# Building gate one-hots token by token with per-partition scalars, multiplying 256 columns at once, and adding the halves on VectorE

## The reference, cut to what matters

```python
def block(hb):                       # per token: 8 heads, 16 experts each = 128 picks
    ...
    sc, ci = lax.top_k(cand, PEER_TOPK)
    e = i1[ci // 16] * PEER_NKEYS + i2[ci % 16]      # expert = (first key, second key)
    g = jax.nn.softmax(sc, axis=-1)
    a = jax.nn.gelu(einsum('td,ted->te', hb, u[e]))
    return einsum('te,ted->td', g * a, v[e])
```

## Time and profile before

| | us |
|---|---|
| median of three runs | 2211.7 |
| the profiled execution, its own time | 2211.71 |
| its span, first to last instruction | 2209.8 |
| TensorE busy | 2155.0 |
| VectorE busy | 1125.3 |
| ScalarE busy | 608.4 |
| the 1024 gate products of 128 columns with the high part or the rest, first and last start | 882.4 to 1341.2 |

### The profile page before, as it was taken

One profiled execution on the slowest core, in us unless ns is written; L12 is line 12 of the kernel. 1 busy time (PEld: TensorE's weight loads), 2 busy tenths in 40 slices (PEclk: granted clock), 3 DMA queues, 4 the chain that ended last, 5 costly groups with the idle time before them and its releaser, 6 DMA issues.

```text
span 2209.8 us, 30856 instructions
## 1 busy us (share of the span) xinstructions
PE 2155.0 (98%) x12924; PEld 1464.6 (66%) x12924; DVE 1125.3 (51%) x2470; ACT 608.4 (28%) x1026; POOL 180.9 (8%) x272
## 2 busy tenths in 40 slices
PE   6999999989899999999999999999999999999999
PEld 4733435668688888898898988888444444444444
DVE  4197636452687993555554442230554554554452
ACT  0102122210123233333333333232233233233231
POOL 0001000000054650000000000000400000000000
PEclk9999969559999999999999999999999999999999
DMA  3232512001121343444444444542967667556551
GB/s 139 79 84 95 185 43 91 1 3 58 39 77 44 130 173 116 173 173 192 191 192 192 191 173 188 187 162 108 323 192 241 207 199 236 200 183 227 199 182 39
DMA packets 131690, 326.21 MB, mean 148 GB/s; under 512 B 22888, under 2 KB 88664, under 8 KB 115168
## 3 DMA queue, kind: packets, MB, share of 16 engines
q1 hardware_dynamic: 128080, 316.34, 40.1%
q0 software_dynamic: 3472, 7.91, 1.5%
HBM read 250.95 MB, written 73.27 MB: 147 GB/s over the span
## 4 chain that ended last, share of the span: by engine, by line
PE 96%; DVE 3%; DMA 1%; ACT 0%; issue 0%; SPq 0%; DVEq 0%; ACTq 0%
PE psum L1696 31%; PE psum L1741 29%; PE psum L1465 27%; PE psum L1717 5%; PE psum L1534 1%; PE psum L1471 1%; DMA g_in<-d_gate 0%; DVE sdm L1089 0%; DMA xT<-in_xT 0%; DVE v_lo L1388 0%; DVE rstd L846 0%; DVE mtmp L845 0%; DVE mtmp L844 0%; DVE hraw L1118 0%; DVE w_f L1397 0%
## 5 line engine op out<-in xcount | busy, mean ns | idle before, releaser
L1696 PE MATMUL psum<-h_hi,u_hi 128*128 128x260 bf16 x2048 | 395.1, 274 | 0.7 <-ACT Ssb L752 0.7
L1696 PE MATMUL psum<-h_lo,u_hi 128*128 128x260 bf16 x2048 | 393.7, 273 | 0.0
L1696 PE MATMUL psum<-h_hi,u_lo 128*128 128x260 bf16 x2048 | 393.5, 273 | 0.0
L1741 PE MATMUL psum<-w_hi,v_hi 128*128 128x512 bf16 x1024 | 388.1, 379 | 1.2 <-DVE w_lo L1404 1.2
L1741 PE MATMUL psum<-w_hi,v_lo 128*128 128x512 bf16 x1024 | 388.1, 379 | 0.0
L1741 PE MATMUL psum<-w_lo,v_hi 128*128 128x512 bf16 x1024 | 388.1, 379 | 0.0
L1255 DVE TENSOR_TENSOR u_lo<-u_raw,u_hi 128x1024 bf16<-128x1024 f32 x128 | 152.5, 1218 | 367.0 <-ACT u_hi L760 367.0
L1397 DVE TENSOR_TENSOR w_f<-a_in,g_in 128x512 f32<-128x512 f32 x128 | 87.9, 686 | 297.6 <-PE psum L1741 245.9
L1696 PEld LDWEIGHTS psum<-h_hi,u_hi 128*128 128x128 bf16 x2048 | 200.4, 98 | 29.7 <-issue 0.8
L1696 PEld LDWEIGHTS psum<-h_lo,u_hi 128*128 128x128 bf16 x2048 | 198.1, 97 | 31.0
L1696 PEld LDWEIGHTS psum<-h_hi,u_lo 128*128 128x128 bf16 x2048 | 198.2, 97 | 30.8
(11 more groups left out here) (311 smaller groups left out, 2175.8 us busy)
## 6 DMA issues: line engine op xcount, KB each, us to landing
u_raw<-in_uT SPq DMA_DIRECT2D x32, 2048.0 KB, 10.3
v_raw<-in_v SPq DMA_DIRECT2D x32, 2048.0 KB
d_act<-act_f SPq DMA_DIRECT2D x32, 1024.0 KB, 4.8
d_gate<-stage SPq DMA_DIRECT2D x16, 2048.0 KB, 6.3
a_in<-d_act SPq DMA_DIRECT2D x32, 1024.0 KB
g_in<-d_gate SPq DMA_DIRECT2D x32, 1024.0 KB
wr<-in_w SPq DMA_DIRECT2D x13, 2048.0 KB, 7.7
kv<-in_ck SPq DMA_DIRECT2D x24, 256.0 KB, 4.3
```

The lines of the kernel that those rows point to most:

```text
L1696: mm = pe.matmul(upair[n % 2][:, f, 0:HALF], w[g % 2][:, k, c * P:(c + 1) * P], hs[:, k, halves[f]], start=(k == 0 and x == 0), stop=(k == ...
L1741: mm = pe.matmul(ybank[m], w[g % 2][:, c, m * P:(m + 1) * P], z[g % 2][:, c, :], start=(g == 0 and c == 0 and x == 0), stop=(g == NG - 1 a ...
```

## The change

Three things are rewritten. VectorE builds each one-hot for one token with TENSOR_SCALAR: the 128 keys along the row (`keyrow`, bf16), compared with a column of `tables` (now f32) as a per-partition scalar, and for `gateL` multiplied by a second per-partition scalar. That is three instructions of 128 columns a token, 24 a pair, instead of four of 1024. The outputs are packed, so that TensorE reads its operands without a stride, and high part and rest lie side by side: one product of 256 columns a token, 8 a pair instead of 16 of 128. The two halves are no longer added by accumulation in PSUM. A quad now takes two banks, `gate_parts` gives its halves, ScalarE copies the high half into `stage`, and VectorE adds the other half in place (`add_gate_parts`), GATE_LAG = 2 loop indices behind. There are now two bank pairs, and quad q waits for the add of quad q - 2. `gl_ev` is signalled by VectorE. AT_V moves from 96 to 98.

```diff
-AT_V = 96
+AT_V = 98
+GATE_LAG = 2
...
-    gateL = [put(f"gateL{b}", [P, 2, 2, P, 4], BF16, ...
-    oneL = [put(f"oneL{b}", [P, 2, P, 4], BF16, ...
+    tables = put("tables", [P, 4, SEQ], F32, D0)
+    keyrow = put("keyrow", [P, P], BF16, c0 + 1024)
+    gateL = [put(f"gateL{b}", [P, 8, 2, P], BF16, ...
+    def gate_parts(q):
+        pair = pa[:, 4 + 2 * (q % 2):6 + 2 * (q % 2), :]
+        return pair.rearrange("p j (t x e) -> p x e (j t)", t=2, x=2)
...
-                A(stage[n % 2][:, :, at:at + 4], gbank[q % 4].rearrange("p (t e) -> p e t", t=4), ACT.Copy
-                  ).then_inc(gl_ev, 1)
+                A(stage[n % 2][:, :, at:at + 4], gate_parts(q)[:, 0, :, :], ACT.Copy).then_inc(gl_high, 1)
...
             def gate_rows(u):
-                each = lambda row: tables[:, row, 8 * u:8 * u + 8].rearrange(...)
-                tt(oneL[u % 2][:, :, :, :], keys, each(0), ALU.is_equal).then_inc(gl_one, 1)
+                row = lambda x, t: tables[:, x, 8 * u + t:8 * u + t + 1]
                 if u >= PRING:
                     v.wait_ge(gl_mm, 2 * (u - PRING + 1))
-                tt(oneR[u % PRING][:, :, :, :], keys, each(1), ALU.is_equal).then_inc(gl_R, 1)
-                v.wait_ge(gl_one, u + 1)
-                for part in range(2):
-                    tt(gateL[u % PRING][:, part, :, :, :], oneL[u % 2][:, :, :, :], each(2 + part), ALU.mult
-                       ).then_inc(gl_L, 1)
+                for t in range(8):
+                    ts(oneR[u % PRING][:, t, :], keyrow[:, :], row(1, t), None, ALU.is_equal)
+                    ts(gateL[u % PRING][:, t, 0, :], keyrow[:, :], row(0, t), row(2, t), ALU.is_equal, ALU.mult)
+                    ins = ts(gateL[u % PRING][:, t, 1, :], keyrow[:, :], row(0, t), row(3, t), ALU.is_equal, ALU.mult)
+                ins.then_inc(gl_L, 1)
+
+            def add_gate_parts(q):
+                n = q // QUADS
+                v.wait_ge(gl_high, q + 1)
+                at = 4 * (q % QUADS)
+                part = stage[n % 2][:, :, at:at + 4]
+                tt(part, part, gate_parts(q)[:, 1, :, :], ALU.add).then_inc(gl_ev, 1)
...
                 if 0 <= n - AT_GATES < NPAIRS:
                     gate_rows(n - AT_GATES)
+                if 0 <= n - AT_GATES - GATE_LAG < NPAIRS:
+                    add_gate_parts(2 * (n - AT_GATES - GATE_LAG))
+                    add_gate_parts(2 * (n - AT_GATES - GATE_LAG) + 1)
...
             def gates(q):
-                if q >= 4:
-                    pe.wait_ge(gl_ev, q - 3)
+                if q >= 2:
+                    pe.wait_ge(gl_ev, q - 1)
                 for t in range(4):
-                    for part in range(2):
-                        mm = pe.matmul(gbank[q % 4][:, t * P:(t + 1) * P], oneR[u % PRING][:, q % 2, :, t],
-                                       gateL[u % PRING][:, part, q % 2, :, t], start=(part == 0), stop=(part == 1))
+                    at = (t % 2) * 2 * P
+                    mm = pe.matmul(gbank[2 * (q % 2) + t // 2][:, at:at + 2 * P], oneR[u % PRING][:, 4 * (q % 2) + t, :],
+                                   gateL[u % PRING][:, 4 * (q % 2) + t, :, :], start=True, stop=True)
```

More of the change, by code:

```diff
@@ L158, in trunk_and_peer @@
     c0 = hs0 + HT
-    tables = put("tables", [P, 4, SEQ], BF16, c0)
     s_int = put("s_int", [DB * H, 3, TOPK], U32, c0 + 4160)
@@ L285, in trunk_and_peer @@
     act_f = [put(f"act_f{b}", [P, GC, NT], F32, C0 + 8320 * b) for b in range(2)]
-    keys4 = put("keys4", [P, P, 4], BF16, D0)
-    gateL = [put(f"gateL{b}", [P, 2, 2, P, 4], BF16, E0 + 4096 * b) for b in range(PRING)]
-    oneL = [put(f"oneL{b}", [P, 2, P, 4], BF16, E0 + 16384 + 2048 * b) for b in range(2)]
+    tables = put("tables", [P, 4, SEQ], F32, D0)
+    g_high = put("g_high", [P, SEQ], BF16, c0)
+    keyrow = put("keyrow", [P, P], BF16, c0 + 1024)
+    gateL = [put(f"gateL{b}", [P, 8, 2, P], BF16, E0 + 4096 * b) for b in range(PRING)]
     T0 = F0 + 8192
     stage = [put(f"stage{b}", [P, NKEYS, TB], F32, T0 + 16384 * b) for b in range(2)]
-    oneR = [put(f"oneR{b}", [P, 2, P, 4], BF16, T0 + 32768 + 2048 * b) for b in range(PRING)]
+    oneR = [put(f"oneR{b}", [P, 8, P], BF16, T0 + 32768 + 2048 * b) for b in range(PRING)]
     assert T0 + 32768 + 2048 * PRING <= W0
@@ L344, in trunk_and_peer @@
     qz_zero, s_used, rank_steps, one_hot, looked = sems("qz_zero scores_used rank_steps one_hot_ranks looked_up")
-    keys_set, tb_made, tb_read, gl_one, gl_L, gl_R, gl_mm, gl_ev = sems(
-        "keys_set tb_made tb_read gl_one gl_L gl_R gl_mm gl_ev")
+    keys_set, tb_made, tb_read, gl_L, gl_mm, gl_high, gl_ev = sems(
+        "keys_set tb_made tb_read gl_L gl_mm gl_high gl_ev")
     g_stored, a_stored, as_stored = ([sem(f"{n}{b}") for b in range(2)] for n in ("g_stored", "a_stored", "as_stored"))
@@ L1342, in _ @@
                 v.wait_ge(tb_made, i + 1)
-                v.tensor_copy(tables[:, 2, t], bk[:, 2 * P:3 * P]).then_inc(tb_high, 1)
-                v.tensor_copy(tables[:, 0, t], bk[:, 0:P])
-                v.tensor_copy(tables[:, 1, t], bk[:, P:2 * P])
+                v.tensor_copy(g_high[:, t], bk[:, 2 * P:3 * P]).then_inc(tb_high, 1)
+                v.tensor_copy(tables[:, 0:3, t], bk[:, 0:3 * P].rearrange("p (x t) -> p x t", x=3))
                 v.wait_ge(tb_high, i + 1)
-                tt(tables[:, 3, t], bk[:, 2 * P:3 * P], tables[:, 2, t], ALU.subtract).then_inc(tb_read, 1)
+                tt(tables[:, 3, t], bk[:, 2 * P:3 * P], g_high[:, t], ALU.subtract).then_inc(tb_read, 1)
             n64 = DB * H
@@ L1368, in _ @@
             v.wait_ge(hs_done, KT)
-            do(v.tensor_copy(keys4[:, :, :], iota.unsqueeze(2).to_broadcast([P, P, 4])), keys_set)
-            keys = keys4[:, :, :].unsqueeze(1).to_broadcast([P, 2, P, 4])
+            do(v.tensor_copy(keyrow[:, :], iota), keys_set)
             def gate_rows(u):
-                each = lambda row: tables[:, row, 8 * u:8 * u + 8].rearrange(
-                    "p (q t) -> p q t", q=2).unsqueeze(2).to_broadcast([P, 2, P, 4])
-                tt(oneL[u % 2][:, :, :, :], keys, each(0), ALU.is_equal).then_inc(gl_one, 1)
+                row = lambda x, t: tables[:, x, 8 * u + t:8 * u + t + 1]
                 if u >= PRING:
                     v.wait_ge(gl_mm, 2 * (u - PRING + 1))
-                tt(oneR[u % PRING][:, :, :, :], keys, each(1), ALU.is_equal).then_inc(gl_R, 1)
-                v.wait_ge(gl_one, u + 1)
-                for part in range(2):
-                    tt(gateL[u % PRING][:, part, :, :, :], oneL[u % 2][:, :, :, :], each(2 + part), ALU.mult
-                       ).then_inc(gl_L, 1)
+                for t in range(8):
[9 more added lines that the diff above has]
+                tt(part, part, gate_parts(q)[:, 1, :, :], ALU.add).then_inc(gl_ev, 1)
             def v_low(g, s):
@@ L1710, in gates @@
                 if q % 2 == 0:
-                    pe.wait_ge(gl_R, u + 1)
-                    pe.wait_ge(gl_L, 2 * (u + 1))
-                if q >= 4:
-                    pe.wait_ge(gl_ev, q - 3)
+                    pe.wait_ge(gl_L, u + 1)
+                if q >= 2:
+                    pe.wait_ge(gl_ev, q - 1)
                 for t in range(4):
-                    for part in range(2):
-                        mm = pe.matmul(gbank[q % 4][:, t * P:(t + 1) * P], oneR[u % PRING][:, q % 2, :, t],
-                                       gateL[u % PRING][:, part, q % 2, :, t], start=(part == 0), stop=(part == 1))
+                    at = (t % 2) * 2 * P
+                    mm = pe.matmul(gbank[2 * (q % 2) + t // 2][:, at:at + 2 * P], oneR[u % PRING][:, 4 * (q % 2) + t, :],
+                                   gateL[u % PRING][:, 4 * (q % 2) + t, :, :], start=True, stop=True)
                 mm.then_inc(gl_mm, 1)
```

## The result

| | before | after |
|---|---|---|
| median, us | 2211.7 | 2315.8 (2312.7 to 2327.3) |
| the profiled execution, its own time | 2211.71 | 2315.89 |
| its span | 2209.8 | 2314.0 |
| TensorE busy | 2155.0 | 2114.8 |
| VectorE busy | 1125.3 | 1359.1 |

The changed kernel takes 1.050 times as long, with a 95% interval of 1.044 to 1.056. By the last row the stage grew by 118.6 us, and the whole by only 104.2. Executions of the kernel before take either 2191 to 2198 us or 2205 to 2212, those of the changed kernel 2313 to 2316 or, once, 2327, and the profiled ones are a long one before and a short one after.

What follows compares the result with a forecast made beforehand. TensorE, busy 98%, was taken to set the pace. Rounds 114.4, start 15.6 and end -0.5 summed to 129.5 us, on 2211.7 giving 2341; range 2280 to 2430, chance 0.81.

Steps and rivals of the forecast that it cites:

- S: VectorE's one-hots for a pair: 8 instructions with one scalar and 16 with two, 5.04 us, against 2.40 before.
- D: One VectorE index: subtraction 1.15, one-hots 5.04 and two adds of 0.60, 7.39 us, slower than TensorE's step of 6.27.
- the standstill: TensorE idle before its gates once in four steps, until VectorE's add ends: 1.78 + 1.15 + 5.04 + 0.69 = 8.66 us.
- rounds' surplus: Between first and last pause, 14 rounds of four steps at 37.25 us against 29.08, 8.17 more each: 114.4 us.
- if both hold together: VectorE's one-hots: one source and bf16 each halve column time, giving spacings 0.170 and 0.230; 0.033 more if only one holds.
- The start and the end together: Stage edges: reaching the gates of step 31 costs 15.6 us more, the three steps after step 87 take 0.5 less.
- The wait that is added: TensorE's gates wait for VectorE's add two indices later, behind `u_low` and 24 `gate_rows` instructions: 8.66 us once in four steps.
- The clock: After each pause TensorE runs about 4.7 us at half clock, losing 2.35 us, hidden in the rounds by VectorE's slower pace.
- Dearer pieces: Rival: VectorE's new instructions or adds cost more; S of 5.84 gives 2390 us, 7.44 gives 2490; range 2375 to 2490, chance 0.22.
- cheap ones: Rival: VectorE's scalars are hidden, S = 2.64, TensorE sets the pace outside pauses; 2277 us, range 2250 to 2310, chance 0.13.
- faster: Rival: VectorE's add is done before TensorE asks, so TensorE keeps its 64 us saving: 2148 us, chance 0.03.
- the fixed 0.084 us: On VectorE, an instruction starts 0.084 us before the one ahead has ended; used to turn durations into spacings.

Runs made afterwards that it cites:

- the smaller S: Changed kernel, but from the fifth pair on the low half of `gateL` isn't built, 16 instructions a pair instead of 24: 2284.0 us, ratio 1.037.
- half-and-half kernel: Changed kernel with GATE_LAG = 1, `u_low` later at every fourth index, even quads 256 columns and an add, odd quads accumulated in PSUM: 2171.3 us, ratio 0.985.
- the four that only accumulate: Changed kernel with two 128-column products a token accumulated in PSUM, no adds: 2175.6 us; also with `u_low` later 2137.9, strided weights 2180.2, strided moving operand 2236.8.

## Why the prediction was right, point by point

The forecast was 2341 us, and 2315.8 was measured: the right sign, and 25 us too high. The named places and terms of the argument all appeared, nearly all a little smaller.

| term | forecast | measured | from |
|---|---|---|---|
| gates block | 0.90 | 0.87 | 890.19 above |
| one-scalar, two-scalar spacing | 0.170, 0.230 | 0.16, 0.225 | 1015.39, 1015.55, 1015.78, 1016.00 |
| S, 24 instructions | 5.04 | 4.87 | 1015.39 to 1020.26 |
| an add, apart | 0.60 | 0.595 | 1020.26 to 1021.45, two |
| D, a VectorE index | 7.39 | 7.20 | 1014.25 to 1021.45 |
| the standstill | 8.66 | 8.61 | 1012.47 to 1021.08 |
| its pieces | 1.78 + 1.15 + 5.04 + 0.69 | 1.78 + 1.14 + 4.87 + 0.82 | 1012.47, 1014.25, 1015.39, 1020.26, 1021.08 |
| gates and `up` after it | 8.6 | 8.39 | 1021.08 to 1029.47 |
| gates and `up` before it | 1.05 + 5.37 | 6.32 | 1006.15 to 1012.47 |
| a round | 37.25 | 36.53 | 984.55 to 1021.08 |
| `u_high` waited for, a round | about 8 | 7.65 | 1014.25 |
| rounds' surplus, 14 | 114.4 | 104.3 | 14 x (36.53 - 29.08) |
| stage in all | 129.5 | 118.6 | first gelu to last |

The prediction counts the standstill from when TensorE could have started its next product. The last two products of `up` ahead of it are this row of TensorE's timeline:

```profile
1012.25 0.38 PE L1707 MATMUL psum<-h_hi,u_lo 128*128 128x260 bf16 x2
```

They start 0.112 us apart, so the next could have started at 1012.47. The 8.45 us in the brackets count from 1012.63, where the trace has the last product's end.

**Where the 25 us are.** The first 10.9 are in the stage, and nearly all of them in the rounds. The 24 instructions were sized 0.17 us too long, and S stands four times in a round: 4 x 0.17 = 0.68 of the 0.72 by which a round is shorter. That was the step "if both hold together, 128 bf16 columns stream as long as 64 f32 ones": the case was right, and the duration taken from one row of 254 ns was too coarse. The rest of the 0.72 nearly cancels: gates and `up` before the standstill are 0.10 shorter, the subtractions and adds 0.07, and TensorE starts 0.82 us after the add's start and not 0.69, which is 0.13 longer. The start and the end together were forecast at 15.6 - 0.5 = 15.1 and took 118.6 - 104.3 = 14.3.

The other 14.4 us are not of the change. The first gelu of the changed kernel stands at 721.49 and that of the kernel before at 736.43. This early part ran at another clock; this is the stretch from 300 to 350 us, before and after (length; busy of the engines; granted clock; DMA). The kernel before:

```profile
300.00:350.00 50.00, 50.00 (x140) 20.25 (x139) 25.99 (x76) 9.36 (x31) 0.00 (x0) 0.66 0.20 64
```

The changed kernel:

```profile
300.00:350.00 50.00, 50.00 (x208) 22.61 (x207) 33.65 (x97) 12.64 (x41) 0.00 (x0) 1.00 0.20 64
```

It is not the code that sets it. With the smaller S, whose early part is that of the changed kernel, this stretch is at 0.72 and the first gelu at 733.49. The stretch is at 1.00 with GATE_LAG = 1, with the adds first and in the half-and-half kernel as well, and at 0.66 or 0.67 in the four that only accumulate. Against the shortest of the three times of the kernel before, 2194.89 us, the changed kernel's 2315.8 is 121 us more, about what the stage says. What decides the clock of the early part is open. The prediction took the profiled time as the base and named no such term; a range for it of 15 us downwards would have belonged there.

**The wait that is added** was the core, and it held. TensorE stood idle at 16 places, as forecast (the first at step 28, then 15). The four runs on it bracket the mechanism: with the add an index earlier the pause goes, without S ahead of the add it is shorter by S (3.59 us are left), with eight of its 24 instructions missing it is shorter by 8.45 - 6.67 = 1.78, those instructions' own 8 x 0.225, and being faster than TensorE on the average doesn't remove it.

**The clock** behaved much as the earlier trace rows had it. TensorE's granted clock in stretches of 2 us around the pause:

```profile
1012.00:1014.00 2.00, 0.63 (x6) 0.30 (x4) 0.00 (x0) 1.33 (x2) 0.00 (x0) 1.00 0.00 0
1014.00:1016.00 2.00, 0.00 (x0) 0.00 (x0) 1.75 (x5) 2.00 (x3) 0.00 (x0) 0.83 0.00 0
...
1022.00:1024.00 2.00, 2.00 (x11) 1.39 (x10) 2.00 (x9) 1.19 (x2) 0.00 (x0) 0.50 0.97 393
1024.00:1026.00 2.00, 2.00 (x13) 1.44 (x11) 2.00 (x11) 0.00 (x0) 0.00 (x0) 0.61 0.95 393
1026.00:1028.00 2.00, 2.00 (x20) 1.75 (x18) 2.00 (x9) 0.00 (x0) 0.00 (x0) 1.00 0.90 367
```

TensorE's clock falls from 2.4 to 1.2 GHz at about 1015.3 us, while it stands idle (0.83 is the mean of that stretch; the three left out are at 0.50), stays there through the rest of the idle time and the first 4.5 us of work, and is 2.4 GHz after that. It cost nothing in the rounds, as said: in the round that begins at 984.55 TensorE again waits 0.72 us at 1006.15, for the first of VectorE's two adds, which began at 1005.33.

**The rivals.** Dearer pieces and cheap ones both fell by the same rows: S = 4.87 is nearer to 5.04 than to 5.84 or 2.64, and an add is 0.595 apart, so the stride in PSUM is free for VectorE too. The groups of VectorE have the adds as

```profile
L1390 DVE TENSOR_TENSOR stage<-stage,psum 128x512 f32<-128x512 f32 x128 | 81.7, 679 | 0.4 <-ACT stage L784 0.4
```

which is 679 ns with the stride against 686 for a read of PSUM without one. The price that the Trainium skill, "Vector Engine (DVE) Microarchitecture Reference", measured stream behaviour, has for a source in SBUF that hops by 4 KiB at every element (1.73 ns a column) was not met here, with the source in PSUM. The Trainium skill, "VectorE: DVE Perf Modes", perf-mode tier table, has TENSOR_SCALAR on bf16 in SBUF at four elements a cycle. The measured spacings fit that: they are just under the 0.170 and 0.230 worked out for it, and the next slower case was 0.033 above. They don't prove it, since the part of an instruction that isn't streaming was not measured alone. The rival "faster" needed 24 instructions in 0.4 us and had 4.87.

**What the prediction didn't see.** It priced the 1.00 us that TensorE saves by the count of the products, 16 that become 8, and did not ask what the packing gives alone. The size was right, since it was read from the products of `up`. The reason was not: nearly all of it (0.96) is the packed moving operand. That didn't move the forecast, since the change does both. It hides the better kernel, though: the adds were the price for a width that buys 0.02 us a step.

## What to carry to other kernels

An engine's list is in order, so a wait on it holds everything behind it: put the instruction that another engine needs ahead of one that waits, and count the work for later steps that stands between the two. Being faster on the average step doesn't help if in one step of four its work stands behind a wait that ends only after the other engine was ready. And before an accumulation is moved from PSUM to VectorE, measure the product itself with its operands packed.

## What was not expected of the hardware

The stride of the moving operand, 8 bytes between bf16 elements, doubled a product of 128 columns (0.116 against 0.056 us), while the same stride in the weights left the block at 1.07 against 1.05. The Trainium skill, "Advanced Engine Details and Errata", memory cachelines, says that at least two hits on a line of 16 bytes are needed to absorb the latency of an access. This stride has two hits on a line, and by the measurement they are not enough for TensorE's moving operand.

VectorE's writes at that stride are dearer, though less than their duration says. Its timeline in the kernel with the strided moving operand, where `gateL` is written with the stride and `oneR` packed:

```profile
1006.45 0.43 DVE L1382 TENSOR_SCALAR gateL<-keyrow,tables 128x128 bf16<-128x128 bf16 x1
1006.71 0.43 DVE L1383 TENSOR_SCALAR gateL<-keyrow,tables 128x128 bf16<-128x128 bf16 x1
1006.96 0.25 DVE L1381 TENSOR_SCALAR oneR<-keyrow,tables 128x128 bf16<-128x128 bf16 x1
```

An instruction lasts 0.12 us longer than with packed writes (0.43 against 0.31 above), but the next one starts only 0.03 us later (0.255 apart against 0.225). So the overlap of two instructions is not the fixed 0.084 us of the prediction, and a duration less 0.084 is no safe stand-in for the spacing where the write has a stride.
